# A fifth place for a split weight granule behind the token stages of a two-layer backbone

## The chip, the cores and the metric

One core of a Trainium2 chip runs the whole program. The metric is the device time of one execution in microseconds (us); lower is better. Between two kernels a difference under about 0.2% cannot be told from none here.

## The reference, cut to what matters

```python
def conv_ffn(h, w_in, conv_w, w_out):
    g, v = jnp.split(h @ w_in, 2, axis=-1)
    g = dwconv(g, conv_w)                    # three taps along the tokens
    return (jax.nn.silu(g) * v) @ w_out

for l in range(DEPTH):                       # DEPTH = 2; layer 0 even, layer 1 odd
    ...
    y, yc = even_mixer(...) if l % 2 == 0 else odd_mixer(...)   # input product, mixers, output product
    x = x + mod[2] * rms_norm(y, mix_post_g[l])
    h = modulate(rms_norm(x, ffn_pre_g[l]), mod[3], mod[4])
    x = x + mod[5] * rms_norm(conv_ffn(h, ffn_w_in[l], ffn_conv_w[l], ffn_w_out[l]), ffn_post_g[l])
    ...                                      # the 256 context tokens likewise, in layer 0 alone
```

All is float32: D_MODEL 1024, 512 latent and 256 context tokens, feed-forward width 2816. Layer 0 works on 768 tokens, layer 1 after its input product on 512.

## The kernel before

**Products in three terms.** Each float32 operand is split into a high part in the format fp32r and a low part, the rest. A product is high*high + high*low + low*high on TensorE. The split of a weight granule (128 partitions x 1024 numbers, 512 KB) takes two instructions: ScalarE copies `raw` into `w_hi` (`take_high`, L1089, semaphore `w_high`), then VectorE subtracts into `w_lo` (`take_low`; its instruction is recorded under the helper `vt`, L1506, as all VectorE tensor_tensor work; semaphore `w_low`, `low` in the code).

**Places.** Loads land in two raw buffers: granule n in `raw[:, n % 2]`. The split parts have four places, granule n in number n % 4. So three things are ordered: `load(n)` on the SP queue waits until the low part of n-2 is taken; `take_high(n)` must come behind the last product that read granule n-4; TensorE waits for `low` before it uses n. SP, ScalarE and VectorE go through the granules strictly in order, between their other work.

**Units.** A unit is a product of 256 output columns over all of D_MODEL; it uses two granules (part 0 and part 1, four k-tiles each) and one of two PSUM sets. `product` (L670) runs a unit over all tokens. Feed-forward units come in pairs: the gate half g (copied to `gpad`, then three taps on VectorE, L1967 and L1965) and the value half v (multiplied in, split into `hid_hi`, `hid_lo`). In `ffn` each engine does, for a pair: copy and taps, then the split of the two granules of the next pair's first unit (`unit_high(n + 4)`, `unit_low(n + 4)`), then the other half, then two more granules.

**Token stages and edges.** `token_products` (L724) computes an output product: tokens on the partitions, two halves `a` of 512 columns, `half` = 4 granules each (3 for down02 and down12). Four of these stages are edges: out0, down02, out1, down12. In the second half of an edge TensorE goes tile by tile (128 tokens); behind each tile ScalarE squares, VectorE normalizes, adds to x, normalizes again (`xn`, L1561), TensorE transposes (`turn`, L710), and ScalarE and VectorE modulate and split into `h_hi`, `h_lo`. GpSimd takes part at down02 and down12 (L2155). The next product begins before the last tiles are through: `first_products` (L696) takes the first two units of the next phase (up00, in1, up10) in token segments of 256: segment 0 for unit 0, a `turn`, segment 0 for unit 1, then segment 1 for both, and so on. All four granules of these two units must stay in their places to the last segment.

**Order of the splits at an edge.** With n the edge's first granule, `edge` on ScalarE and VectorE takes granule n + half + 3 between the two halves. When the last tile comes, it takes the next two (n + half + 4 and + 5), ahead of that tile's squares and sums. Behind the last tile's sums it takes the rest, to n + 2 half + 3. At out0 and out1 the four granules of up00 (up10) are n + 8 to n + 11, so their first two are taken at the last tile and the others behind it. At down02 the first granule of in1 is n + half + 3 already, the second and third are taken at the last tile, the fourth behind it. The third unit's granules (up00 + 4 and + 5) follow in `ffn`, behind the first unit's taps.

Of the kernel before, what the change touches and what calls it, by code (L numbers as in the profile page):

```python
# [34 lines left out]
P = 128  # L35
# [87 lines left out]
def token_stages():  # L123
# [3 lines left out]
    for name, nt, ktiles in (("out0", NT, KD), ("down00", NT, 8), ("down01", NT, 8), ("down02", NT, 6),  # L127
# [27 lines left out]
SEGMENTS = (((0, 0, 1, None), (0, 1, 3, FIRST), (1, 0, 1, SECOND), (1, 1, 3, THIRD), (2, 0, 1, FOURTH), (2, 1, 2, None)),  # L155
            tuple((g, 0, size // 2, None) for g, size in enumerate(FFN_GROUPS)))
TokenStage = namedtuple("TokenStage", "nt half edge tiles granules sums squares chain")
# [34 lines left out]
def build(nc, a, out):  # L192
# [3 lines left out]
    with ctx:  # L196
# [30 lines left out]
        W_LO = at[0]  # L227
        w_lo = place("w_lo", [P, 4, 4, 256], F32R)
        ident = place("ident", [P, P])
        ones = place("ones", [P, P])  # L230
# [11 lines left out]
        ada_w = place("ada_w", [P, 4, 2, 512])  # L242
        ada_acc = place("ada_acc", [P, 512])
        A0 = at[0]
        ARENA = top // 32 * 32 - A0
        assert ARENA >= 83960, ARENA

# [39 lines left out]
        ada_m = place("ada_m", [P, 2, 4, 256], offset=RAW)  # L287
        ada_c = place("ada_c", [P, 3, 512], offset=A0 + 36864)
        ada_d = place("ada_d", [P, 512], offset=SCR + 8192)
        ada_r = place("ada_r", [P, 512], offset=SCR + 8192)  # L290
        sums_even = [[ada_acc[:, :], ada_c[:, 0, :]], [ada_c[:, 1, :], ada_c[:, 2, :]]]
        sums_of = [ada_acc[:, :], ada_d[:, :]]
# [66 lines left out]
        w_ffn_out = [a["ffn_w_out"][l].rearrange("(k p) n -> p k n", p=P) for l in range(2)]  # L359
        w_ada = [a["ada_w"][l].rearrange("(k p) n -> p k n", p=P) for l in range(2)]  # L360

        def bank(s_, m, h):
# [315 lines left out]
        def first_products(pe, u, n, rhs, segs, ready, between):  # L678

            for e, (t0, t1) in enumerate(segs):  # L680
                for x in range(2):
                    s = (u + x) % 2
                    if not e:
                        psum_free(pe, u + x)
                    for part in range(2):
                        m_ = n + 2 * x + part
                        if not e:
                            pe.wait_ge(low, m_ + 5)
                        if not x and not part:
                            ready(e)  # L690
                        for kk in range(4):
                            k = 4 * part + kk
                            for m in range(2):
                                c = slice(m * P, (m + 1) * P)
                                for q, (w, x_) in enumerate(((w_hi, rhs[0]), (w_hi, rhs[1]), (w_lo, rhs[0]))):
                                    last = nc.tensor.matmul(acc[:, s, m, t0:t1], w[:, m_ % 4, kk, c], x_[:, k, t0:t1],  # L696
                                                            start=(k == 0 and q == 0), stop=(k == KD - 1 and q == 2))
                    if e == len(segs) - 1:
                        last.then_inc(unit_done, 1)
                    between(2 * e + x)  # L700
# [379 lines left out]
        def _(act):  # L1080
# [3 lines left out]
            def take_high(n, i=0):  # L1084

                if n >= N_GRANULES:
                    return
                act.wait_ge(raw_full[n % 2], loaded(n, i))
                nc.scalar.activation(w_hi[:, n % 4], raw[:, n % 2], ACT.Copy).then_inc(high, 1)  # L1089

# [66 lines left out]
            def edge(name, l, comp):  # L1157
# [9 lines left out]
                granule_used(act, name, half - 1)  # L1167
                take_high(n + half + 3)
                act.wait_ge(y_eps, EDGES.index(name) + 1)
                for j in range(nt):  # L1170
                    if j == nt - 1 and on:
                        for g in range(2):
                            granule_used(act, name, half + g)
                            take_high(n + half + g + 4)
                    y_squares(name, 1, j)
                    q = t.chain + j
                    act.wait_ge(y_square, t.squares + nt + j + 1)
                    nc.scalar.activation(yroot[:, 0, j:j + 1], ysq[:, j, 1:2], ACT.Sqrt, bias=ysq[:, j, 0:1]).then_inc(y_root, 1)
                    if not on:
                        continue  # L1180
                    if j >= behind:
                        tile_half(name, j - behind, l, comp)
                    act.wait_ge(x_new, q + 1)
                    x_squares(j, NT + q, junk_x[:, :])
                    if j >= behind:
                        tile_high(name, j - behind)
                if on:
                    for g in range(2, half):
                        granule_used(act, name, half + g)
                        take_high(n + half + g + 4)  # L1190
                    for j in range(nt - behind, nt):
                        tile_half(name, j, l, comp)
                        tile_high(name, j)
# [199 lines left out]
            def ffn(l, tokens):  # L1393
# [4 lines left out]
                for g, off, count, chunks in SEGMENTS[l]:  # L1398
                    with turns(act, count) as i:
                        u, n, pair = U[f"up{l}{g}"] + 2 * off, G[f"up{l}{g}"] + 4 * off, first_pair + sum(FFN_GROUPS[:g]) // 2 + off  # L1400
                        psum_full(act, u, i)

# [5 lines left out]
                        last.then_inc(set_free[u % 2], 1)  # L1408
                        unit_high(n + 4, i)
                        u, n = u + 1, n + 2  # L1410
# [90 lines left out]
        def _(dve):  # L1501
# [31 lines left out]
            def take_low(n, i=0):  # L1533

                if n < N_GRANULES:
                    dve.wait_ge(high, n + 1 + 4 * i)
                    vt(w_lo[:, n % 4], raw[:, n % 2], w_hi[:, n % 4].bitcast(F32), ALU.subtract).then_inc(low, 1)

# [96 lines left out]
            def edge(name, l, comp, rows_in):  # L1635
# [14 lines left out]
                for j in range(nt):  # L1650
                    summed(name, 2, 0, j)
                take_low(n + half + 3)
                dve.wait_ge(y_square, t.squares + nt)
                nc.vector.tensor_scalar(ysq[:, 0:nt, 0], ysq[:, 0:nt, 0], EPS, None, ALU.add).then_inc(y_eps, 1)
# [3 lines left out]
                for j in range(nt):  # L1658
                    if j == nt - 1 and on:
                        unit_low(n + half + 4)  # L1660
                    summed(name, 2, 1, j)
# [26 lines left out]
                if not mixer:  # L1688
                    nc.vector.memset(poolw[:, :, :], 0.0).then_inc(sem("poolw_zero"), 1)
                    normed(nt - 1)  # L1690
                    tile_low(name, nt - 3)
                for m in range(2, half):
                    take_low(n + half + m + 4)
                for j in range(nt - (1 if mixer else 2), nt):
# [244 lines left out]
            def ffn(l, tokens):  # L1939
# [5 lines left out]
                for g, off, count, chunks in SEGMENTS[l]:  # L1945
                    tile, pair = sum(FFN_GROUPS[:g]) + 2 * off, FT // 2 * l + sum(FFN_GROUPS[:g]) // 2 + off
                    with turns(dve, count) as i:
                        sd.loop(i, 5 + 4 * len(chunks or ()))
                        u, n = U[f"up{l}{g}"] + 2 * off, G[f"up{l}{g}"] + 4 * off
                        if chunks:  # L1950
                            dve.wait_ge(unit_done, u + 2 * i)
                            for e in range(2):
                                ada_sums(chunks[e], sums_of[e:], i)
                        psum_read(dve, u, i)
                        for w in range(3):
                            for m in range(2):
# [13 lines left out]
                                else:  # L1970
                                    sd.done(ins)
                        unit_low(n + 4, i)
                        u, n = u + 1, n + 2
# [227 lines left out]
```

## Time and profile before

| | us |
|---|---|
| median of 3 runs | 1716.85 |
| lowest, highest | 1715.59, 1717.81 |
| profiled execution, its own time | 1718.76 |
| span of its instructions | 1717.0 |

The profiled execution lies 1.91 above the median of the runs. TensorE is busy for 1625.7 us of the span, VectorE for 1023.8, ScalarE for 555.2, GpSimd for 54.7. Its mean granted clock is 0.977 of full speed. Windows and timelines are in us from the start of the span.

### The profile page before, as it was taken

To read this page: it belongs to the slowest core of one execution; us is meant where nothing else is said; L and a number is where in the kernel's file an instruction comes from. 1 tells how busy PE (TensorE), PEld (TensorE's weight loads), DVE (VectorE), ACT (ScalarE), POOL (GpSimd) and SP (SyncE) were. 2 spreads that over 40 slices of the span, in tenths; PEclk is the share of its full clock that TensorE was granted. 3 is DMA by queue.
4 is the path that set the end of the run, shared out by engine and by line. 5 is a ranking of instruction groups with operands and counts; after the bars stand their busy time and mean duration, and the time that the engine had idled before them with its cause. 6 is when DMAs were issued, how large, how long until landed. Compare 5 with 4: busy or idle time off the path is not lost.

```text
span 1717.0 us, 21965 instructions
## 1 busy us (share of the span) xinstructions
PE 1625.7 (95%) x8698; PEld 1358.3 (79%) x8698; DVE 1023.8 (60%) x1448; ACT 555.2 (32%) x883; POOL 54.7 (3%) x74
## 2 busy tenths in 40 slices
PE   6999999886899999999999999899899999999998
PEld 2688887675788887888888887788677888888886
DVE  2899995653675766467734444754783644344344
ACT  2313215472262321023210323631433543233233
POOL 0400000110000000000000000100000000000001
PEclk9999999988899999999999999899999999999999
DMA  9422221304314454444424132131001233233222
GB/s 300 137 62 69 59 70 44 130 25 86 111 50 147 147 168 162 132 161 161 160 85 148 50 98 62 65 99 49 25 1 50 74 98 111 86 98 111 75 95 87
DMA packets 134009, 169.43 MB, mean 99 GB/s; under 512 B 15970, under 2 KB 92450, under 8 KB 133930
## 3 DMA queue, kind: packets, MB, share of 16 engines
q1 hardware_dynamic: 133360, 168.11, 30.8%
q8 instruction: 55, 0.90, 0.2%
q10 hardware_dynamic: 570, 0.22, 0.1%
q14 instruction: 24, 0.20, 0.0%
HBM read 166.17 MB, written 2.15 MB: 98 GB/s over the span
## 4 chain that ended last, share of the span: by engine, by line
PE 81%; DVE 8%; ACT 4%; issue 2%; DMA 1%; POOL 1%; POOLq 0%; DVEq 0%; SPq 0%; ACTq 0%
PE acc L670 47%; PE acc L724 19%; PE acc L696 3%; PE acc L875 2%; PE acc L1071 2%; PE acc L1050 2%; PE acc L776 1%; DVE w_lo L1506 1%; PE acc L1018 1%; PE acc L641 1%; PE acc L910 1%; DVE y L1506 1%; DMA ada_w<-in_ada_w 1%; DVE x L1673 1%; POOL y L2155 1%
## 5 line engine op out<-in xcount | busy, mean ns | idle before, releaser
L670 PE MATMUL acc<-h_hi,w_hi 128*128 128x512 f32 (+1 forms) x1424 | 417.7, 354 | 7.4 <-DVE w_lo L1506 4.4
L670 PE MATMUL acc<-h_lo,w_hi 128*128 128x512 f32 (+1 forms) x1424 | 412.8, 351 | 0.0
L670 PE MATMUL acc<-h_hi,w_lo 128*128 128x512 f32 (+1 forms) x1424 | 412.2, 351 | 0.0
L1506 DVE TENSOR_TENSOR w_lo<-raw,w_hi 128x1024 fp32r<-128x1024 f32 x186 | 222.8, 1229 | 155.7 <-ACT w_hi L1089 155.7
L1089 ACT ACTIVATE w_hi<-raw 128x1024 fp32r<-128x1024 f32 x186 | 189.1, 1055 | 259.3 <-PE acc L724 222.7
L670 PEld LDWEIGHTS acc<-h_hi,w_hi 128*128 128x128 f32 x1424 | 230.5, 189 | 45.2 <-DVE w_lo L1506 4.8
L670 PEld LDWEIGHTS acc<-h_lo,w_hi 128*128 128x128 f32 x1424 | 231.3, 189 | 39.4 <-issue 0.5
L670 PEld LDWEIGHTS acc<-h_hi,w_lo 128*128 128x128 f32 x1424 | 229.8, 189 | 38.3
L724 PE MATMUL acc<-w_hi,hid_hi 128*128 128x512 f32 x440 | 175.7, 399 | 0.0
L724 PE MATMUL acc<-w_hi,hid_lo 128*128 128x512 f32 x440 | 175.0, 398 | 0.0
L724 PE MATMUL acc<-w_lo,hid_hi 128*128 128x512 f32 x440 | 175.0, 398 | 0.0
L1774 DVE SCALAR_TENSOR_TENSOR conv_u<-conv_u,dw_w 128x783 f32<-128x783 f32 x120 | 124.1, 1034 | 4.0
L1967 DVE TENSOR_SCALAR hid<-gpad,ffn_cw 128x512 f32 (+1 forms) x66 | 25.2, 438 | 131.1 <-ACT gpad L1407 131.1
L724 PEld LDWEIGHTS acc<-w_hi,hid_lo 128*128 128x128 f32 x440 | 83.2, 189 | 20.4
L724 PEld LDWEIGHTS acc<-w_lo,hid_hi 128*128 128x128 f32 x440 | 83.3, 189 | 20.0
L724 PEld LDWEIGHTS acc<-w_hi,hid_hi 128*128 128x128 f32 x440 | 83.2, 189 | 19.9
L1506 DVE TENSOR_TENSOR hid<-hid,acc 128x1024 f32 (+2 forms) x22 | 32.7, 1488 | 107.8 <-ACT mods L1105 59.5
L1965 DVE SCALAR_TENSOR_TENSOR hid<-gpad,ffn_cw,hid 128x512 f32 (+3 forms) x132 | 77.5, 656 | 0.0
L1105 ACT ACTIVATE mods<-acc,vec 128x1 f32 (+2 forms) x72 | 14.5, 262 | 191.4 <-PE acc L641 191.1
L696 PE MATMUL acc<-h_hi,w_hi 128*128 128x256 f32 x224 | 65.9, 294 | 10.7 <-DVE w_lo L1506 9.3
L724 PE MATMUL acc<-w_hi,h_hi 128*128 128x512 f32 x160 | 65.5, 409 | 6.0 <-DVE small L1937 3.3
L1527 DVE SCALAR_TENSOR_TENSOR ada_acc<-ada_w,cond,ada_acc 128x512 f32<-128x512 f32 x91 | 68.2, 750 | 4.0
(234 smaller groups left out, 2048.6 us busy)
## 6 DMA issues: line engine op xcount, KB each, us to landing
ada_w<-in_ada_w SPq DMA_DIRECT2D x88, 512.0 KB, 5.8
raw<-in_ffn_w_in SPq DMA_DIRECT2D x88, 512.0 KB, 3.7
raw<-in_ffn_w_out SPq DMA_DIRECT2D x44, 512.0 KB, 4.5
raw<-in_even_w_in SPq DMA_DIRECT2D x24, 512.0 KB, 4.5
ada<-in_ada_w SPq DMA_DIRECT2D x8, 1024.0 KB, 12.1
raw<-in_odd_w_in SPq DMA_DIRECT2D x12, 512.0 KB, 3.9
raw<-in_even_w_out SPq DMA_DIRECT2D x8, 512.0 KB, 4.7
ada_m<-in_ada_w SPq DMA_DIRECT2D x8, 512.0 KB, 3.9
```

Source lines behind the costliest of these rows:

```text
L670: last = nc.tensor.matmul(acc[:, s, m, t0:t1], w[:, slot, kk, c], x_[:, k, t0:t1], start=(k == 0 and q == 0), stop=(k == KD - 1 and q == 2))
L696: last = nc.tensor.matmul(acc[:, s, m, t0:t1], w[:, m_ % 4, kk, c], x_[:, k, t0:t1], start=(k == 0 and q == 0), stop=(k == KD - 1 and q == 2))
L724: last = nc.tensor.matmul(tile_bank(name, a, j), x_[:, k, j * P:(j + 1) * P], w[:, m_ % 4, 2 * kk:2 * kk + 2, :].rearrange("p a c -> p (a ...
L875: last = nc.tensor.matmul(dst, probs[e % 4][:, t * P - t0:t * P - t0 + P], v_tok[:, ORDER[q], hd, :], start=(q, d, t) == FIRST_TOUCH[b], s ...
L1050: last = nc.tensor.matmul(acc[:, 0, n % 2, t0:t1], inb[:, 2 + hd, i * P:(i + 1) * P], kT[:, hd // 3, t0:t1], start=True, stop=True)
L1071: last = nc.tensor.matmul(acc[:, 1, 1, c:c + P], v1[:, j, (hd // 3) * HD:(hd // 3 + 1) * HD], pT[:, n % 2, j * P:(j + 1) * P], start=(j == ...
L1089: nc.scalar.activation(w_hi[:, n % 4], raw[:, n % 2], ACT.Copy).then_inc(high, 1)
L1506: return nc.vector.tensor_tensor(out_, in0, in1, op)
L1527: ins = nc.vector.scalar_tensor_tensor(of[e], w, scale, of[e], ALU.mult, ALU.add)
L1774: ins = nc.vector.scalar_tensor_tensor(dst, src, tap, dst, ALU.mult, ALU.add)
L1965: ins = nc.vector.scalar_tensor_tensor(dst, src, c, dst, ALU.mult, ALU.add)
L1967: ins = nc.vector.tensor_scalar(dst, src, c, None, ALU.mult)
```

## The change

A fifth place `w_edge` (high and low part) is added beside the four. Three granules, the set `early`, use it: the first of up00, the second of in1, the first of up10. Each is taken between the two halves of its edge, right behind granule n + half + 3. At the last tile the edge then takes the granules n + half + 5 up to n + 2 half + 2 (two at out0 and out1, one at down02), and one behind the last tile. As up00's and up10's first granule does not stand in the four places, the third unit's first granule has its place free while the first pair is at work; `ffn` takes it ahead of its first pair's work, and only the third unit's second granule is left behind the taps. To make room `ada_acc` moves over scratch space, `sums_even` lies wholly in `ada_c`, and the program's dynamic_dma_scratch_size goes from 8192 to 1024.

```diff
-            tuple((g, 0, size // 2, None) for g, size in enumerate(FFN_GROUPS)))
+            ((0, 0, 1, None), (0, 1, FFN_GROUPS[0] // 2 - 1, None))
+            + tuple((g, 0, size // 2, None) for g, size in enumerate(FFN_GROUPS) if g))
...
+        w_edge = place("w_edge", [P, 2, 4, 256], F32R)
...
-        ada_acc = place("ada_acc", [P, 512])
...
-        ada_c = place("ada_c", [P, 3, 512], offset=A0 + 36864)
-        ada_d = place("ada_d", [P, 512], offset=SCR + 8192)
+        ada_c = place("ada_c", [P, 4, 512], offset=A0 + 36864)
+        ada_acc = place("ada_acc", [P, 512], offset=SCR + 6176)
+        ada_d = place("ada_d", [P, 512], offset=SCR + 8224)
...
-        sums_even = [[ada_acc[:, :], ada_c[:, 0, :]], [ada_c[:, 1, :], ada_c[:, 2, :]]]
+        sums_even = [[ada_c[:, 2 * q + e, :] for e in range(2)] for q in range(2)]
...
+        early = {G["up00"], G["in1"] + 1, G["up10"]}
+
+        def w_of(n):
+
+            return (w_edge[:, 0], w_edge[:, 1]) if n in early else (w_hi[:, n % 4], w_lo[:, n % 4])
...
                 granule_used(act, name, half - 1)
                 take_high(n + half + 3)
+                if on:
+                    take_high(n + half + 4)
                 act.wait_ge(y_eps, EDGES.index(name) + 1)
                 for j in range(nt):
                     if j == nt - 1 and on:
-                        for g in range(2):
+                        for g in range(1, half - 1):
                             granule_used(act, name, half + g)
                             take_high(n + half + g + 4)
...
-                    for g in range(2, half):
-                        granule_used(act, name, half + g)
-                        take_high(n + half + g + 4)
+                    granule_used(act, name, 2 * half - 1)
+                    take_high(n + 2 * half + 3)
...
+                        if n in early:
+                            take_high(n + 4)
                         psum_full(act, u, i)
...
                         last.then_inc(set_free[u % 2], 1)
-                        unit_high(n + 4, i)
+                        if n not in early:
+                            take_high(n + 4, i)
+                        take_high(n + 5, i)
...
                 take_low(n + half + 3)
+                if on:
+                    take_low(n + half + 4)
...
                     if j == nt - 1 and on:
-                        unit_low(n + half + 4)
+                        for m in range(1, half - 1):
+                            take_low(n + half + m + 4)
...
-                for m in range(2, half):
-                    take_low(n + half + m + 4)
+                take_low(n + 2 * half + 3)
...
+                        if n in early:
+                            take_low(n + 4)
                         psum_read(dve, u, i)
...
-                        unit_low(n + 4, i)
+                        if n not in early:
+                            take_low(n + 4, i)
+                        take_low(n + 5, i)
...
-    nc = bacc.Bacc("TRN2", target_bir_lowering=False, num_devices=1, dynamic_dma_scratch_size=8192)
+    nc = bacc.Bacc("TRN2", target_bir_lowering=False, num_devices=1, dynamic_dma_scratch_size=1024)
```

`first_products`, `take_high` and `take_low` now address the places through `w_of`. The SP queue's code is unchanged.

## Rows read from the trace of the kernel before

**Rows 1.** TensorE's waits over the span: total us, times, longest

```profile
PE acc L651 <- DVE ada_d L1527: 9.9, 2, 7.7
PE acc L696 <- DVE w_lo L1506: 9.3, 5, 3.9
PE acc L670 <- DVE w_lo L1506: 4.4, 2, 2.7
```

**Rows 2.** Chain that ended last around out0 and up00: start, us, what

```profile
497.09 2.27 DVE w_lo L1506 x2
...
503.19 0.75 DVE xn L1561
...
505.08 1.15 DVE w_lo L1506
506.36 23.29 PE acc L696 x192
...
536.91 1.15 DVE w_lo L1506
...
538.10 18.75 PE acc L670 x96
...
575.17 17.06 PE acc L670 x96
```

**Rows 3.** Timeline, up00's third unit, TensorE and the gate copy before it

```profile
529.72 1.51 ACT L1407 ACTIVATE gpad<-acc 128x1024 f32<-128x1024 f32 x2 [20.00 <-PE acc L696]
538.10 0.50 PE L670 MATMUL acc<-h_hi,w_hi 128*128 128x512 f32 x1 [2.71 <-DVE w_lo L1506]
```

**Rows 4.** Windows of up00's third unit, its own matmuls: us, busy (x), clock, DMA share, GB/s

```profile
538.50:541.90 3.40, 3.40 (x13) 2.92 (x12) 0.50 0.67 208
541.90:545.30 3.40, 3.40 (x21) 2.93 (x20) 1.00 1.02 346
```

**Rows 5.** Timeline between the halves of out0 (VectorE, ScalarE) and of out1 (ScalarE)

```profile
463.47 0.16 DVE L1654 TENSOR_SCALAR small<-small 128x6 f32<-128x6 f32 x1
465.35 0.60 ACT L1147 ACTIVATE junk<-acc 128x512 f32<-128x512 f32 x1 [7.01 <-PE acc L724]
...
1320.58 0.60 ACT L1147 ACTIVATE junk<-acc 128x512 f32<-128x512 f32 x1 [3.85 <-PE acc L724]
```

**Rows 6.** Timeline at up10, TensorE behind two of its waits, and the gate copy

```profile
1348.90 0.35 PE L696 MATMUL acc<-h_hi,w_hi 128*128 128x256 f32 x1 [1.16 <-DVE w_lo L1506]
1362.04 1.03 ACT L1407 ACTIVATE gpad<-acc 128x1024 f32<-128x1024 f32 x1
1368.06 0.50 PE L670 MATMUL acc<-h_hi,w_hi 128*128 128x512 f32 x1 [1.66 <-DVE w_lo L1506]
```

**Rows 7.** Timeline at down02, the splits of in1's four granules, and TensorE

```profile
1059.45 1.23 DVE L1506 TENSOR_TENSOR w_lo<-raw,w_hi 128x1024 fp32r<-128x1024 f32 x1 [1.74 <-ACT w_hi L1089]
1095.12 2.36 DVE L1506 TENSOR_TENSOR w_lo<-raw,w_hi 128x1024 fp32r<-128x1024 f32 x2 [2.16 <-ACT w_hi L1089]
1096.40 0.58 PE L696 MATMUL acc<-h_hi,w_hi 128*128 128x256 f32 x1 [3.93 <-DVE w_lo L1506]
1106.18 1.22 DVE L1506 TENSOR_TENSOR w_lo<-raw,w_hi 128x1024 fp32r<-128x1024 f32 x1
1107.45 0.39 PE L696 MATMUL acc<-h_hi,w_hi 128*128 128x256 f32 x1 [1.85 <-DVE w_lo L1506]
```

**Rows 8.** Chain that ended last through down02

```profile
1060.76 4.21 DVE y L1506 x7
```

**Rows 9.** Windows at in1: us, PE, PEld, DVE, ACT, POOL, clock, DMA, GB/s

```profile
1096.40:1101.70 5.30, 5.29 (x25) 5.30 (x26) 4.16 (x7) 2.42 (x7) 2.30 (x1) 0.50 0.73 227
1107.45:1112.00 4.55, 4.54 (x25) 4.55 (x26) 2.45 (x5) 1.06 (x1) 0.00 (x0) 0.62 0.70 233
```

**Rows 10.** Window of the program's start, columns as in rows 9

```profile
10.00:42.00 32.00, 25.00 (x123) 12.18 (x123) 11.48 (x22) 10.91 (x26) 0.00 (x0) 1.00 1.01 325
```

**Rows 11.** DMA issues of the whole span: count, KB each, median us to landing

```profile
raw<-in_ffn_w_in SPq DMA_DIRECT2D x88, 512.0 KB, 3.7
```

More of the change, by code:

```diff
@@ L242, in build @@
         ada_w = place("ada_w", [P, 4, 2, 512])
-        ada_acc = place("ada_acc", [P, 512])
         A0 = at[0]
         ARENA = top // 32 * 32 - A0
-        assert ARENA >= 83960, ARENA
+        assert ARENA >= 84000, ARENA
         qkov = place("qkov", [P, 16, T], offset=A0)
@@ L694, in first_products @@
                                 c = slice(m * P, (m + 1) * P)
-                                for q, (w, x_) in enumerate(((w_hi, rhs[0]), (w_hi, rhs[1]), (w_lo, rhs[0]))):
-                                    last = nc.tensor.matmul(acc[:, s, m, t0:t1], w[:, m_ % 4, kk, c], x_[:, k, t0:t1],
+                                for q, (w, x_) in enumerate(((0, rhs[0]), (0, rhs[1]), (1, rhs[0]))):
+                                    last = nc.tensor.matmul(acc[:, s, m, t0:t1], w_of(m_)[w][:, kk, c], x_[:, k, t0:t1],
                                                             start=(k == 0 and q == 0), stop=(k == KD - 1 and q == 2))
@@ L1088, in take_high @@
                 act.wait_ge(raw_full[n % 2], loaded(n, i))
-                nc.scalar.activation(w_hi[:, n % 4], raw[:, n % 2], ACT.Copy).then_inc(high, 1)
+                dst = w_of(n)[0]
+                nc.scalar.activation(dst, raw[:, n % 2], ACT.Copy).then_inc(high, 1)
             def unit_high(n, i=0):
@@ L1536, in take_low @@
                     dve.wait_ge(high, n + 1 + 4 * i)
-                    vt(w_lo[:, n % 4], raw[:, n % 2], w_hi[:, n % 4].bitcast(F32), ALU.subtract).then_inc(low, 1)
+                    hi, lo = w_of(n)
+                    vt(lo, raw[:, n % 2], hi.bitcast(F32), ALU.subtract).then_inc(low, 1)
             def unit_low(n, i=0):
```

## Prediction

> **What bounds the kernel now.** I read the page first: TensorE is busy for 1625.7 of the 1717.0 us, so only its waits and the stretches at its lower clock can be won back. Then its waits [rows 1]: for the low part of a weight granule it waits 9.3 us in five places in `first_products` and 4.4 us in two in `product`; the other large one there (`ada_d`, the sums for adaLN columns) this edit does not touch. The timelines at the three edges show where they are. At up00 the wait ahead of the second unit is seen in the chain: low part at 505.08, TensorE on at 506.36 [rows 2], behind 1.2 us of idleness (the `turn` was over at about 505.2); a like wait stands before the first unit. Then comes 2.71 us ahead of the third unit [rows 3]. At up10 they are 1.16 ahead of the second unit and 1.66 ahead of the third [rows 6]; the first unit has the fifth of the five, 9.3 - 1.2 - 1.16 - 3.93 - 1.85 = 1.2. At in1 they are 3.93 in the middle of unit 0 and 1.85 in the middle of unit 1 [rows 7]. The windows give the clock: right behind the 2.71 us wait TensorE is granted 0.50 (the 1.2 GHz level) for 3.4 us, with 13 matmuls of one of the three terms where the next 3.4 us at 1.00 (2.4 GHz) hold 21 [rows 4]; at in1 it is 0.50 behind the 3.93 us wait and 0.62 behind the 1.85 us wait [rows 9].
>
> **The change at up00.** (1) up00's first granule is split right behind out0's last. Cost: one ScalarE copy (about 1.05) and one subtraction (1.15, [rows 2]) between the halves. VectorE had put the epsilon in at 463.47, and ScalarE began the second half's squares at 465.35, when TensorE delivered the tile [rows 5]: the cover is 465.35 - 463.47 - 0.16 = 1.7 us, so 1.15 costs nothing; without that cover it would cost 1.15. (2) At the last tile two granules are split as before, now the second and third. The last tile's squares, sums and `xn` (ready at 503.19 + 0.75 = 503.94, [rows 2]) keep their times. Unit 0 may begin 1.2 earlier, at about 497.1, but its 48 matmuls end by 502.9, and then the `turn` of the last tile waits for `xn` at 503.94. Before, that turn began at 504.16; so of the first 1.2 us only 0.15 is kept, which I leave out. (3) The third granule is there by 499.4, so unit 1 begins when the turn is over: the 1.2 us wait at 506.36 is gone. Unit 1 needs the fourth granule 2.9 us later, at about 508.1; it is now alone behind `xn` and `h_lo`, ready at 505.08 + 1.15 = 506.2 [rows 2]. Gain 1.2. (4) From there TensorE runs through to the end of segment 2 (535.4 before). The third unit's first granule is taken by both engines at the start of `ffn`, some 25 us ahead; its load needs place 0 of `raw`, free at 499.4, and lands within about 3.7 us [rows 11]. The PSUM set is free when the gate copy ends, 529.72 + 1.51 = 531.2 [rows 3], 4 us ahead. So the 2.71 us go. The second granule stays behind the taps: 536.91 before, one place earlier and shifted by 1.2 with TensorE, ready near 536.9; the unit reaches it after half its 16.75 us, near 542.6. Gain 2.7. (5) The clock: with no idleness from 505 on there is nothing for the fall at 538.5 to follow. At the full clock the 13 matmuls take 13/21 of 3.4 = 2.1, so the stretch costs 3.4 - 2.1 = 1.3 by this count; by time at half the clock it is 1.7. The unit took 18.75 us against 17.06 for the next pair's first [rows 2], a difference of 1.7, and I take that. Sum at up00: 1.2 + 2.7 + 1.7 = 5.6.
>
> SP's queue: granules load in the old order, only sooner: the third by 34 us, as the first's low part now falls in the pause, the fourth by 1.1, the third unit's second half by about 30. The two loads behind the taps come about 1.2 (one subtraction) and 1.2 (TensorE's shift) earlier, and the adaLN weights behind them with them. From here to down02 TensorE has one wait, in down00 (9.9 - 7.7 = 2.2 us, [rows 1]), for VectorE's sums for the adaLN columns, which begin behind TensorE's own last unit and so move with it. So the 5.6 us reach down02 whole.
>
> **At up10**, the same with 4 tiles: between the halves of out1 ScalarE stands idle for 3.85 us [rows 5], more than the copy and the subtraction one after the other (2.2). The wait of 1.16 goes; the wait of 1.66 goes, since the gate copy ends at 1362.04 + 1.03 = 1363.1 [rows 6] and TensorE reaches the third unit at 1368.06 - 2.8 = 1365.2. The wait ahead of the first unit is again taken up by the turn of the last tile. Gain 1.16 + 1.66 = 2.8. The clock stayed at 1.00 there, nothing to win. In the following pair the load of the third unit's fourth granule is issued when the taps are over, as before, and is not waited for. TensorE has no wait from 1368 to the last product.
>
> **At down02 and in1** the cover is missing. The chain runs through the very place where the second granule is now put: low part of the first at 1059.45, then the gating product at 1060.76 [rows 7, 8] (seven pieces without a pause), and from there through ScalarE, GpSimd and VectorE tile by tile to 1101. The subtraction moves all of this by 1.15. In exchange, at the last tile one granule is split and not two (1095.12, 2.36 for the two, [rows 7]), which gives 1.13 back ahead of the last sum: everything behind it, and the fourth granule at 1106.18, keeps its time. TensorE now runs through the first 3.93 us wait, but then waits for `xn` of the next-to-last tile, computed behind that last sum, and at last for the same fourth granule: unit 1's second part begins at 1107.45 as before. Gain 0. Its last wait grows from 1.85 to about 4.6 us, so the low clock behind it comes as before [rows 9]: 24 matmuls in 4.5 us where 2.9 would do, both times. Bounds: -1.6 if the clock stays up this time, +1.7 if one more stretch of 3.4 us at 0.50 falls behind 1107.45, +1.15 more if the last tile does not give back its part.
>
> **Other parts.** The places of `ada_acc`, `ada_c`, `ada_d` are scratch of other stages at times when those are over; no instruction is added: 0. Reading `w_edge` and not `w_hi` in the same matmuls: 0 (what TensorE does per matmul has no term for the place in any row). The smaller DMA scratch: see the last rival.
>
> **Sum.** 5.6 + 2.8 + 0 = 8.4 us. Against the profiled execution, 1718.76 - 8.4 = 1710.4; the median of the runs lies 1.91 lower, 1716.85 - 8.4 = **1708.4**.
>
> The Trainium skill, "TensorE: Matmul & The Clock Gate", section on what is actually happening, says that the gate's watching is not tied to the kernel's start, so where the clock turns varies from run to run. This trace, being one, can neither show nor deny it. By that rule the 1.7 us at up00 was lost in some runs of the median only, and the gain would be between 6.7 and 8.4.
>
> **Rivals.** (a) *The clock takes part of it back.* Shifted by 5.6 us, the idle stretches at in1 (now some 2.7 and 4.6 us) and the one in down00 meet the clock otherwise: one or two further stretches of 1.7 us, or the 1.7 at up00 not won in the median. For it: the drops behind waits of 1.85 and 2.71 us [rows 4, 9]. Time: 8.4 - 1.7 to 8.4 - 3.4 less than before, 1710.1 to 1711.8. (b) *in1 gains too*: somewhere the chain from 1060.76 to 1095 has slack, the 1.15 is absorbed, and the last tile starts 1.13 earlier, with the lower clock of [rows 9] gone: another 1.1 + 1.6, 1705.7. Against it: the chain passes without a pause of its own. (c) *The third unit does not start earlier*: not the split but the taps' neighbour, the freeing of the set or a load not landed, holds it. Then only the two waits of 1.2 go, 2.4 us, 1714.5, within 0.2%. Against it: the copy at 531.2 and a load free since 499.4. (d) *Slower, by the DMA scratch*: if the loads' descriptors pass through the scratch, an eighth of it slows all loads. Loads set the pace in the start, 32 us at a DMA share of 1.01 [rows 10]. It decides the sign where they grow by 8.4/32 = 26%; at 50% they cost 16, giving 1716.85 - 8.4 + 16 = 1724.5. Elsewhere a unit of 17 us needs two loads of 3.7 [rows 11] and has room. Against it: the loads are on the hardware queue q1, and GpSimd issues none.
>
> **How the numbers follow.** Forecast 0.60 (its own range 1707.0 to 1710.0: 1.3 against 1.7 for the clock, 0.15 twice for the turns, and the spread of the runs). (a) 0.20, (b) 0.07, (c) 0.07, (d) 0.06. The range reaches to (b) on one side and over (a) on the other with the 1.15 of in1 added: 1705.5 to 1713.0; (c) and (d), 0.13, lie outside. Faster by over 0.2% (3.4 us, what a measurement can tell): forecast, (a), (b) = 0.87. Within: 0.07. Slower: 0.06.
>
> **What would show it.** TensorE's waits for `w_lo`: the two in `product` gone, the ones in `first_products` down from five to one (in1, about 4.6 us), with waits of about 1 us for `xn` ahead of the last turn at up00 and up10. Third unit of up00 with no idle time and 21 matmuls of a term in every 3.4 us. At down02 the gating product 1.15 later, measured from the half's last sum, the last sum of the edge at its old distance. The first 42 us unchanged. Wrong would be: a wait ahead of the third unit named otherwise; in1's fourth granule earlier or later; a longer landing of the loads.

## The result and the profile after

| | before | after |
|---|---|---|
| median of the runs, us | 1717.19 (5) | 1708.19 (5) |
| lowest, highest | 1715.59, 1719.53 | 1707.60, 1709.33 |
| span of the profiled execution | 1717.0 | 1707.6 |

The ratio is 0.9939, 95% interval 0.9926 to 0.9953: faster, and by 9.0 us in the medians, where 8.4 were forecast (1708.4). The two medians divide to 0.9948, which lies inside the interval. In a later measurement, on chip 15, the same kernel took 1708.88 against 1716.86 (0.9956, 0.9941 to 0.9971).

TensorE's waits in the kernel after, over the span (the answer to [rows 1]; total us, times, longest):

```profile
PE acc L659 <- DVE ada_d L1541: 9.0, 2, 6.9
PE acc L718 <- DVE xn L1576: 8.6, 5, 3.1
PE acc L704 <- DVE w_lo L1520: 4.5, 1, 4.5
```

The two waits for `w_lo` in `product` are gone, and of the five in `first_products` (L704 now) one is left. The waits for `xn` in front of a `turn` (L718) have grown and taken up part of them: 8.6 us in five places, where before had 3.0 us in two:

```profile
PE acc L710 <- DVE xn L1561: 3.0, 2, 2.0
```

The chain that ended last, around up00, answers to [rows 2]:

```profile
501.88 0.76 DVE xn L1576
502.64 0.04 issue
502.69 1.09 PE acc L718 x8
503.78 28.80 PE acc L704 x240
532.58 16.96 PE acc L678 x96
```

and the timelines of TensorE's last wait there and of what lies between the halves of out0 (VectorE, ScalarE) answer to [rows 3, 5]:

```profile
502.69 1.09 PE L718 MATMUL acc<-ident,xn 128*128 128x128 f32 x8 [1.16 <-DVE xn L1576]
...
462.13 1.21 DVE L1520 TENSOR_TENSOR w_edge<-raw,w_edge 128x1024 fp32r<-128x1024 f32 x1
463.26 0.16 DVE L1671 TENSOR_SCALAR small<-small 128x6 f32<-128x6 f32 x1
...
464.00 0.60 ACT L1156 ACTIVATE junk<-acc 128x512 f32<-128x512 f32 x1 [6.07 <-DVE small L1671]
```

From the last `turn` on TensorE is one piece to the end of the third unit, 240 matmuls and then 96. The new subtraction of 462.13 is over at 463.34, and VectorE's epsilon behind it at 463.42, ahead of the tile that ScalarE takes at 464.00. The profile names the epsilon for this start, but it had been done for 0.6 us; from TensorE's first matmul of the half to ScalarE's first square it is 1.74 us before and after (465.35 - 463.61 and 464.00 - 462.26). So the cover of 1.7 us held. The third unit's windows (us, TensorE busy, its weight loads, clock, DMA share, GB/s; compare [rows 4]) have no stretch at half the clock:

```profile
536.50:539.90 3.40, 3.40 (x21) 2.94 (x20) 1.00 0.99 304
539.90:543.30 3.40, 3.40 (x21) 2.94 (x21) 1.00 1.02 382
```

At up10 the chain is likewise one piece behind the turn, where [rows 6] had two waits:

```profile
1340.54 1.09 PE acc L718 x8
1341.63 17.28 PE acc L704 x144
1358.91 41.28 PE acc L678 x182
```

At down02 and in1, timeline of VectorE's splits and of TensorE (answers to [rows 7]):

```profile
1050.55 1.23 DVE L1520 TENSOR_TENSOR w_lo<-raw,w_hi 128x1024 fp32r<-128x1024 f32 x1 [1.74 <-ACT w_hi L1098]
1051.70 1.22 DVE L1520 TENSOR_TENSOR w_edge<-raw,w_edge 128x1024 fp32r<-128x1024 f32 x1
...
1090.09 1.09 PE L718 MATMUL acc<-ident,xn 128*128 128x128 f32 x8 [2.51 <-DVE xn L1576]
...
1098.55 0.58 PE L704 MATMUL acc<-h_hi,w_hi 128*128 128x256 f32 x1 [4.51 <-DVE w_lo L1520]
```

The 3.93 us wait of [rows 7] has become one of 2.51 us for `xn`, and the wait for the fourth granule is 4.51 us. From the first granule's low part to unit 1's second part it is 1098.55 - 1050.55 = 48.0 us, as before (1107.45 - 1059.45 = 48.0). The windows around it and in the odd mixer that follows (us; busy and count of TensorE, its weight loads, VectorE, ScalarE, GpSimd; clock, DMA share, GB/s):

```profile
1087.50:1092.00 4.50, 1.99 (x18) 1.92 (x18) 3.70 (x6) 2.41 (x7) 2.00 (x1) 1.00 0.02 5
1098.55:1102.50 3.95, 3.95 (x18) 3.95 (x19) 2.45 (x5) 1.06 (x1) 0.00 (x0) 0.50 0.84 268
1174.50:1177.90 3.40, 3.40 (x10) 2.20 (x10) 0.55 (x2) 0.23 (x1) 0.00 (x0) 0.50 0.02 5
1177.90:1181.30 3.40, 3.40 (x13) 2.54 (x12) 1.85 (x3) 0.00 (x0) 0.00 (x0) 0.50 0.00 0
1201.80:1205.20 3.40, 3.11 (x9) 2.08 (x10) 2.81 (x6) 3.29 (x5) 0.00 (x0) 0.50 0.00 0
```

Behind the wait for `xn` the clock stays at 1.00, behind the one for the granule it is 0.50 (as in [rows 9]), and in the mixer three stretches of 3.4 us stand at 0.50, where the profiled execution of before has one:

```profile
1183.60:1187.00 3.40, 3.40 (x7) 1.43 (x6) 0.55 (x2) 0.23 (x1) 0.00 (x0) 0.50 0.02 5
```

Put together from the start of one stage's first matmul to the next's, in the two profiled executions. "Attention" is here, and in all that follows, the stage from the odd mixer's value product to its first attention scores; the 70.7 us of attention behind it are the same in all traces and stand under "all else".

| stage | before | after | saved |
|---|---|---|---|
| start, layer 0 up to the turns of out0 | 463.61 | 462.26 | 1.35 |
| out0's second half, up00 to unit 1 | 42.75 | 41.28 | 1.47 |
| up00, unit 1 to the third unit | 31.73 | 28.88 | 2.85 |
| third unit and its partner | 36.94 | 35.31 | 1.63 |
| the rest of layer 0's FFN | 456.72 | 455.15 | 1.57 |
| turns of down02, in1 to unit 1's second part | 75.69 | 75.69 | 0.00 |
| the rest of in1 and the projections behind it | 66.19 | 66.56 | -0.37 |
| attention | 48.69 | 51.04 | -2.35 |
| out1's second half, up10 to unit 1 | 55.89 | 54.58 | 1.31 |
| up10, unit 1 to the third unit | 19.17 | 17.36 | 1.81 |
| all else | 419.62 | 419.49 | 0.13 |
| span | 1717.0 | 1707.6 | 9.4 |

Five of the rows with a gain are the prediction's. The 1.57 in the rest of the FFN was not in it, the -2.35 in attention was there as a rival, and the 1.35 of the start is of the size by which executions of one kernel differ there (462.26 and 460.87 us in the two traces of the kernel after).

### The profile page after: what moved, and what is told of

Read it like the earlier page. It is cut to its first block, busy times and chain, and to the rows that moved or that the text cites. A ratio compares the mean times of both kernels' runs of the same rounds, so it can differ in the third digit from the quotient of the medians.

```text
span 1707.6 us, 21913 instructions
## 1 busy us (share of the span) xinstructions
PE 1621.4 (95%) x8698; PEld 1356.7 (79%) x8698; DVE 1023.9 (60%) x1448; ACT 546.3 (32%) x876; POOL 54.3 (3%) x74
## 2 busy tenths in 40 slices
DMA packets 134010, 169.43 MB, mean 99 GB/s; under 512 B 15971, under 2 KB 92451, under 8 KB 133931
## 3 DMA queue, kind: packets, MB, share of 16 engines
q1 hardware_dynamic: 133360, 168.11, 31.1%
## 4 chain that ended last, share of the span: by engine, by line
PE 82%; DVE 7%; ACT 4%; issue 2%; DMA 1%; POOL 1%; POOLq 0%; SPq 0%; DVEq 0%; ACTq 0%
PE acc L678 47%; PE acc L732 19%; PE acc L704 4%; PE acc L883 2%; PE acc L1079 2%; PE acc L1058 2%; PE acc L784 1%; PE acc L1026 1%; PE acc L649 1%; DMA ada_w<-in_ada_w 1%; PE acc L918 1%; DVE w_lo L1520 1%; DVE x L1691 1%; POOL y L2176 1%; DVE y L1520 1%
## 5 line engine op out<-in xcount | busy, mean ns | idle before, releaser
L1520 DVE TENSOR_TENSOR hid<-hid,acc 128x1024 f32 (+3 forms) x22 | 32.7, 1488 | 107.0 <-ACT mods L1114 54.6
L883 PEld LDWEIGHTS acc<-v_tok,probs 128*128 128x128 f32 x336 | 47.2, 221 | 24.4 <-DVE probs L1892 12.3
L1541 DVE SCALAR_TENSOR_TENSOR ada_d<-ada_w,cond,ada_d 128x512 f32<-128x512 f32 x84 | 62.9, 749 | 4.6 <-DMA ada_w<-in_ada_w 2.6
```

The lines of the kernel that those rows point to most:

```text
L883: last = nc.tensor.matmul(dst, probs[e % 4][:, t * P - t0:t * P - t0 + P], v_tok[:, ORDER[q], hd, :], start=(q, d, t) == FIRST_TOUCH[b], s ...
L1520: return nc.vector.tensor_tensor(out_, in0, in1, op)
L1541: ins = nc.vector.scalar_tensor_tensor(of[e], w, scale, of[e], ALU.mult, ALU.add)
```

## The experiments

**Scratch alone.** Does the smaller DMA scratch slow the loads (rival (d)), and does it have a part in layer 0's faster FFN?

```diff
-    nc = bacc.Bacc("TRN2", target_bir_lowering=False, num_devices=1, dynamic_dma_scratch_size=8192)
+    nc = bacc.Bacc("TRN2", target_bir_lowering=False, num_devices=1, dynamic_dma_scratch_size=1024)
```

> The kernel before with nothing changed but dynamic_dma_scratch_size, 8192 to 1024. Theory 1 (the loads do not pass through the scratch): 1717.2 as before, the start from 10 to 42 us at the same DMA share, loads landing in 3.7 us. Theory 2 (they do): slower by 8 us and more, longer landings. Theory 3 (the trace of after has about 1.7 us less in layer 0's units between 540 and 1050 than my sum, because two matmuls of 512 and 256 columns take 347 ns there and not 353; that comes from where things lie in SBUF, which the scratch shifts): about 1715.5, and the units of layer 0's loops take 16.75 and not 17.06.

Measured: 1718.68 against 1717.97, ratio 1.0008 (0.9999 to 1.0017). The start's window, columns as in [rows 10], has the same share and rate:

```profile
10.00:42.00 32.00, 24.84 (x126) 12.26 (x127) 11.48 (x22) 10.79 (x26) 0.00 (x0) 1.00 1.01 325
```

Loads of `in_ffn_w_in` land in 3.6 us (3.7 before, [rows 11]). Rival (d) falls: the scratch shows no cost (the interval leaves room for 0.17%, 2.9 us, where the rival had 8.4 and more), and it gives nothing either; the slower units of layer 0 took 17.06 us as before.
**The third unit's first granule behind the taps again.** The rest of after stays.

```diff
-                        if n in early:
-                            take_high(n + 4)
                         psum_full(act, u, i)
...
-                        if n not in early:
-                            take_high(n + 4, i)
-                        take_high(n + 5, i)
+                        unit_high(n + 4, i)
```

and likewise on VectorE.

> The changed kernel, but the third unit's first granule is split behind the taps again, at up00 and at up10. Theory 1 (the terms of the prediction stand alone): up00's third unit waits about 2.7 us again and the clock falls to 0.50 behind it in most runs (1.7), up10's waits about 1.7: 6.0 us over the changed kernel, 1714.2; only the two waits of 1.2 stay won. Theory 2 (the wait is for the PSUM set or for a load): no change against 1708.2.

Measured: 1711.91, ratio 0.9967 (0.9954 to 0.9979), so 1.9 to 4.8 us above after by the two ratios of after. The wait and the low clock behind it are back at up00 (timeline of TensorE; the granted clock is 0.51 from 533.60 to 537.00):

```profile
532.81 0.62 PE L678 MATMUL acc<-h_hi,w_hi 128*128 128x512 f32 x2 [2.71 <-DVE w_lo L1516]
533.27 0.51 PE L678 MATMUL acc<-h_lo,w_hi 128*128 128x512 f32 x2
533.62 0.80 PE L678 MATMUL acc<-h_hi,w_lo 128*128 128x512 f32 x2
```

Unit 1 to the third unit takes 31.74 us and the next pair 36.93, both as before: together 4.5 us above after, the two terms 2.7 and 1.7 of the prediction. At up10, however, there was no wait, and the stage took 17.63 us, not 19.17. Something else had won that 1.66.

**The loop split alone.** In before's profile a row stands ahead of up10's gate copy that the prediction did not quote, an activation table load of 1.28 us; in after it is gone:

```profile
1360.75 1.28 ACT L1407 ACT_TABLE_LOAD   x1 [8.49 <-PE acc L696]
1362.04 1.03 ACT L1407 ACTIVATE gpad<-acc 128x1024 f32<-128x1024 f32 x1
```

The edit splits the first pair of layer 1 off the loop and does nothing else:

```diff
-            tuple((g, 0, size // 2, None) for g, size in enumerate(FFN_GROUPS)))
+            ((0, 0, 1, None), (0, 1, FFN_GROUPS[0] // 2 - 1, None))
+            + tuple((g, 0, size // 2, None) for g, size in enumerate(FFN_GROUPS) if g))
```

> Before with one edit, the loop split at layer 1 (its first pair of units outside the loop). Theory: the table load at up10 goes and unit 1 to the third unit takes 17.6 us instead of 19.17; layer 0 keeps its 140.93 and 169.74 us; 1717.0 - 1.55 = 1715.5. Rival: the wait there is for the fifth granule alone, 19.17 us stay and the time is 1717.0. Second rival: the faster pairs of layer 0 come from the changed code and not from the layout; then 140.25 us show here too and the time is 1713.8.

Measured: 1717.58 against 1718.41, ratio 0.9994 (0.9981 to 1.0008). By itself the time cannot be told from none; the trace can. ScalarE's timeline in this kernel:

```profile
1359.10 1.03 ACT L1408 ACTIVATE gpad<-acc 128x1024 f32<-128x1024 f32 x1 [8.48 <-PE acc L697]
1360.02 2.00 ACT L1090 ACTIVATE w_hi<-raw 128x1024 fp32r<-128x1024 f32 x2
1362.03 1.28 ACT L1414 ACT_TABLE_LOAD   x1
1363.72 1.06 ACT L1414 ACTIVATE hid<-hid 128x1024 f32<-128x1024 f32 x1 [0.41 <-DVE hid L1966]
```

and in the kernel of the next experiment, which has before's loops:

```profile
1357.41 1.28 ACT L1407 ACT_TABLE_LOAD   x1 [8.49 <-PE acc L696]
1358.71 1.03 ACT L1407 ACTIVATE gpad<-acc 128x1024 f32<-128x1024 f32 x1
1359.63 2.00 ACT L1089 ACTIVATE w_hi<-raw 128x1024 fp32r<-128x1024 f32 x2
1363.65 1.28 ACT L1413 ACT_TABLE_LOAD   x1 [2.02 <-DVE hid L1965]
```

With the split the copy follows TensorE at once, the two splits come 1.28 earlier against the product's end, and the third unit waits no more: 17.62 us for the stage, against 19.17 (the cause of the wait at up10 was the late copy, and with it the late splits). The Trainium skill, "ScalarE: Activation LUTs", section on what a table load costs, gives 1283 ns for the load and about as much again for a drain; here the load has those 1.28 us, but the copy starts 1.30 us behind the load's start and the whole stage gained 1.55, so the second part is not seen. Over the span seven table loads fewer are made (883 ScalarE instructions before, 876 after), all from the two lines of this loop. Layer 0's slower units kept their 17.06 us, so the second rival falls; down01's stage took 141.24 us, 0.3 more than before, all of it in its first unit (16.96 for 16.65), as in the kernel with the scratch alone.

**The ada sums moved alone.** In after six of the units of layer 0's FFN, pairs of matmuls of 512 and 256 columns, are shorter by 0.3 us. The edit moves `ada_acc` and the fourth `ada_c` (and `ada_d` by 32 bytes) as in after; no fifth place, old scratch, old loops:

```diff
-        ada_acc = place("ada_acc", [P, 512])
-        ada_c = place("ada_c", [P, 3, 512], offset=A0 + 36864)
-        ada_d = place("ada_d", [P, 512], offset=SCR + 8192)
+        ada_c = place("ada_c", [P, 4, 512], offset=A0 + 36864)
+        ada_acc = place("ada_acc", [P, 512], offset=SCR + 6176)
+        ada_d = place("ada_d", [P, 512], offset=SCR + 8224)
...
-        sums_even = [[ada_acc[:, :], ada_c[:, 0, :]], [ada_c[:, 1, :], ada_c[:, 2, :]]]
+        sums_even = [[ada_c[:, 2 * q + e, :] for e in range(2)] for q in range(2)]
```

> Before with one edit: ada_acc and the fourth ada_c moved as in after, with no fifth place, the old scratch and the old loops; 2 KB fewer stand ahead of the arena. Theory: the faster pairs of layer 0 (347 ns, down01's stage 140.25 us) come with the places of the ada sums, and the time is 1717.0 - 1.6 = 1715.4. Rival: they come from the addresses of the weights or the hidden matrices, which the fifth place shifts by 8 KB; then 140.93 us and 1717.0 stay.

Measured: 1715.00, ratio 0.9981 (0.9970 to 0.9992). The chain's rows where [rows 2] has a unit of 17.06 us, and of the next unit:

```profile
575.38 16.75 PE acc L670 x96
592.13 0.79 PE acc L641 x8
592.92 16.75 PE acc L670 x96
```

down01's stage took 140.25 us and down02's 169.43, as in after (before: 140.93 and 169.74). The rival, the weights' addresses, falls: the fifth place is not here. The kernels with after's scratch alone and with after's loops alone kept 17.06. The edit also shifts what lies behind `ada_acc` by 2 KB, so whether the place of the sums does it or that shift is open.

**Layout and loops together, nothing early.** After with one edit on the side of the places; the order of the splits at all three edges is that of before (this part of the edit is not shown).

```diff
-        early = {G["up00"], G["in1"] + 1, G["up10"]}
+        early = {}
```

> The memory layout of after (the fifth place, left unused, the moved sums, the small scratch) and its loop split at layer 1, with no granule early. Theory: a row of the profile that the prediction did not have, the activation table load ahead of the gpad copy at up10, goes with the loop split (unit 1 to the third unit there 17.6 us instead of 19.17), and the paired matmuls of layer 0's FFN run at 347 ns instead of 350 to 356 because of where things lie (down01's stage 140.25 us instead of 140.93, down02's 169.43 instead of 169.74). With before at 1717.0 that makes about 1717.0 - 1.6 - 1.6 = 1713.8. Rival: both come with the early granules alone, and this kernel takes 1716.5 to 1717.5 with stages of 19.17 and 140.93 us.

Measured: 1714.94, ratio 0.9973 (0.9964 to 0.9983), with stages of 17.61, 140.25 and 169.43 us. That is 3.5 us less than before in the medians, 4.6 by the ratio and 3.1 (1.56 and 1.57) by the stages. So 3 to 5 of the 9.0 us have nothing to do with when a granule is split.

**One edge early at a time.** Layout and loops of after, and in `early` only up00's granule, only in1's, only up10's, or the two outside in1. The first of these edits; an edge that is not in `early` has the order of before:

```diff
-        early = {G["up00"], G["in1"] + 1, G["up10"]}
+        early = {G["up00"]}
```

> The changed kernel with the fifth place used at up00 alone; down02 and out1 in the order of before. Theory 1 (5.6 of the 8.4 us are at up00): 1717.2 - 5.6 = 1711.6; waits of 1.2, 1.2 and 1.7 us at up10 again. Theory 2 (the clock term is not won in the median, or is made up elsewhere): 1713.3.

> After with the early granule at up10 alone. By the traces so far: out1's turn shorter by 0.9, unit 1 shorter by 0.4, unit 1 to the third unit 17.36 instead of 17.62 (0.26): 1.6 under the layout kernel of this group, so 1713.8 - 1.6 = 1712.2; up00 keeps 34.74 and 31.73 us. The prediction's own sum would have 1.16 + 1.66 = 2.8 from the early granule alone and so 1711.0.

> The changed kernel with the fifth place used at in1 alone; out0 and out1 in the order of before, no third unit early. Theory 1 (in1's edit is worth nothing): 1717.2 less the 1.6 us that up10 gains without its granule, as the run with the third unit late showed (the first pair of layer 1 stands outside the loop and its copy has no table load ahead of it): 1715.6. Theory 2 (the longer idleness of TensorE at in1 costs more clock): 1717 to 1719.

> The changed kernel without in1's early granule: at down02 the order of before, at out0 and out1 the new one. Theory 1 (the subtraction added between the halves is given back at the last tile, and the fourth granule sets in1's time): 1708.2, the same as changed; at in1 waits of 3.9 and 1.85 us as before, and from the first split between the halves to unit 1's second part 48.0 us both times. Theory 2 (in1's edit costs by the longer idleness and the clock): 1706.5. Theory 3 (it gains): 1710 to 1711.

| early | us | ratio (interval) | unit 1 to third unit, up00 / up10 | attention |
|---|---|---|---|---|
| none | 1714.94 | 0.9973 (0.9964 to 0.9983) | 31.73 / 17.61 | 48.70 |
| up00 | 1707.57 | 0.9946 (0.9933 to 0.9960) | 28.87 / 17.62 | 48.21 |
| up10 | 1712.19 | 0.9963 (0.9949 to 0.9977) | 31.72 / 17.36 | 51.07 |
| in1 | 1716.01 | 0.9991 (0.9982 to 1.0000) | 31.73 / 17.61 | 51.07 |
| up00, up10 | 1705.01 | 0.9922 (0.9908 to 0.9935) | 28.87 / 17.35 | 48.69 |
| all three (again) | 1708.88 | 0.9956 (0.9941 to 0.9971) | 28.88 / 17.36 | 51.10 |

The rows "in1" and "all three" were measured on chip 15, the others on chip 13. up00's granule alone took 1707.57 where 1711.6 was expected; the expectation had nothing for layout and loops, which give 3 to 5 us in all of these kernels. up10's met its 1712.2, and in1's came to 1716.01 for 1715.6. up00's granule is worth 0.0027 of the time, 4.6 us, in the ratios and 1.4 + 2.9 + 1.4 = 5.7 in the stages of its trace; up10's 1.7 and 1.5. in1's granule seems to cost: 0.0018 (3.1 us) added to nothing early, and some 0.0026 (the mean of after's two ratios less 0.9922, 4.4 us) added to the other two. By the traces it is 2.8 and 2.7 us, nearly all in attention. The intervals overlap at their ends or nearly touch, and the kernels stood on different chips, so a loss is likely and its size loose. Up to unit 1's second part the sum is the same with it and without it (75.69 and 75.67), as forecast; the loss lies behind.

**The fourth granule of in1 at the last tile too.** The prediction had this granule as what TensorE waits for at in1. At down02 it is now split at the last tile, ahead of the sums, and none behind:

```diff
-                        for g in range(1, half - 1):
+                        for g in range(1, half - (name[:3] == "out")):
...
-                    granule_used(act, name, 2 * half - 1)
-                    take_high(n + 2 * half + 3)
+                    if name[:3] == "out":
+                        granule_used(act, name, 2 * half - 1)
+                        take_high(n + 2 * half + 3)
```

and likewise on VectorE.

> The changed kernel; at down02 the fourth granule of in1 is split at the last tile too, together with the third, not behind the last tile's sums. TensorE has left down02 some 7 us before ScalarE comes to the last tile there, and the granule's load has long landed, so nothing holds it. Theory 1 (only the place in the order keeps in1 waiting): the last sum is 1.15 later, the turn of the next-to-last tile too; unit 1's second part begins some 3 us earlier and no turn waits long; in1's second segment starts about 4 to 5 us earlier, 1703.5. Theory 2 (the last tiles' own chain through GpSimd and VectorE sets the second segment's start whatever the granules do): the added 1.15 ahead of it counts, 1709.3.

> The changed kernel itself, so that the others of this call have it on the same chip. 1708.2; the run without in1's early granule gave 1705.0 on another chip, so in1's edit either costs 2 to 3 us by the clock (then the in1-only kernel shows it as well), or that was chance and this one gives 1705 to 1706 too.

Measured on one chip: 1702.65 (0.9915, 0.9900 to 0.9929) against after's 1708.88 (0.9956), the best of all versions. TensorE's two largest waits that bear on this and its last wait at in1:

```profile
PE acc L659 <- DVE ada_d L1542: 9.3, 2, 7.2
PE acc L718 <- DVE xn L1577: 8.7, 4, 3.6
...
1093.54 1.09 PE L718 MATMUL acc<-ident,xn 128*128 128x128 f32 x8 [3.65 <-DVE xn L1577]
```

No wait for a `w_lo` is left in `product` or `first_products` (one of 1.0 us in `token_products` stays as in before), though the tile's `xn` is one subtraction later. To unit 1's second part it is 73.67 us, 2.0 less; the next stage takes 15.50 and not 17.57 (its low stretch is gone), and attention 48.68 and not 51.10. Only the 2.0 us are sure to be the edit's: the low stretch was missing too in two kernels with the fourth granule late (15.59 us with up00's granule alone and with the sums moved alone), and attention took 48.7 us in others as well.

**And the third granule at out0 and out1 behind the last tile's normalization.** On top of that version:

```diff
-                        for g in range(1, half - (name[:3] == "out")):
+                        for g in range(1, 2 if name[:3] == "out" else half):
...
+                    if j == nt - 1 and name[:3] == "out":
+                        granule_used(act, name, half + 2)
+                        take_high(n + half + 6)
```

and likewise on VectorE.

> As the kernel with in1's fourth granule early, and at out0 and out1 only the second granule of up00 (up10) is split ahead of the last tile's squares and sums; the third one behind that tile's normalization, ahead of the low part of the tile before. Theory 1 (the turn of the last tile waits for the normalization, which stands behind both splits): it comes 1.1 us earlier at either edge, unit 1's granule is there when the turn is over: 2.2 us less than the kernel it is built on, 1701.3. Theory 2 (the granule is then what comes late): the same time as that kernel, the wait named for the low part again.

Measured: 1703.54 (0.9927, 0.9913 to 0.9940). The wait for `xn` ahead of the turn is gone at both edges (from unit 0's first matmul to unit 1's it takes 7.22 us where it took 7.99 at up00, and 6.86 for 7.62 at up10): 1.5 us by the trace, not to be seen in the median beside runs that spread by 8 us (1698.17 to 1706.22). The two kernels cannot be told apart, so neither theory is decided by the time; by the trace theory 1 holds, with 1.5 for its 2.2 us.

## Why the prediction came out, step by step

- **up00, first wait (0.15 left out), second wait (1.2).** Right; together 1.47. The turn for the last tile does wait for `xn`, 1.16 us, as step (2) said.
- **up00, the third unit (2.7).** Right: 2.85, and undoing that one split brought 2.71 back.
- **up00, the clock (1.7).** Right: 1.63. One reading of its rows was wrong without harm: the 13 and 21 of [rows 4] count all matmuls of the stretch, not those of one term. The Trainium skill, "TensorE: Matmul & The Clock Gate", section on what is actually happening, by which the clock's turns vary from run to run, would have made this a gain in some runs only. Here all eight traces with the wait (before's among them) had a stretch at 0.50 and none of the six without it did, so whether the clock fell did not vary at this place; how much it cost did, 1.4 to 2.9 us by the length of the third unit. At in1 the traces bear the rule out (see the last section).
- **The covers between the halves.** Right at out0 and, by the same distances, at out1. No wait for a load came up.
- **up10 (1.16 + 1.66).** The size is right (1.31 and 1.81), the reason only half. The second term was put down to the early granule, while the loop split, which the prediction listed in no step, wins 1.55 of it without any granule early. That the number came out is luck to this extent. With both in, the early granule adds 0.26 there. "no instruction is added: 0" missed that instructions fall away.
- **in1 (0).** Right in mechanism and number to the granule wait; the gating product moved by 1.13 us against the first granule's low part (1052.90 - 1050.55 = 2.35 us for 1060.67 - 1059.45 = 1.22), TensorE's wait for the first tile's `xn` grew from 1.96 to 3.08 us, and the last tile gave it back. The fourth granule set the time, and taking that wait away won 2.0.
- **Other parts (0).** Wrong. Where the sums of the adaLN columns lie, or what that shifts, is worth 1.6 us by the stages and 3.3 by the ratio (1.4 at the least).
- **Rival (a).** It came in beside the forecast, at a place it did not name: not in down00 or in1 but in attention, +2.35 us (in1 itself took 0.37 more). The four traces that have in1's granule early and its fourth one late all show 49.9 to 51.1 us there; of the eight with none early at in1, seven show 48.2 to 48.7; with the fourth moved as well, 48.7 and 47.7. That it is the longer idleness at in1 which brings it about fits this count but is not shown: one kernel without it (up10 alone) had 51.07 too, in an execution that took 1719.17 us, 7.0 above that kernel's median.
- **Rival (b)** fell (75.69 both times), **(c)** fell (no wait ahead of the third unit), **(d)** fell (scratch alone).

So the sum of 8.4 met 9.0 partly by luck: the five terms gave 9.1 instead of 8.4 in the traces, the unforeseen 1.6 and the clock's -2.7 took off 1.1, and the start's 1.35, which is within what executions differ by, put it back. Of the 9.1 some 1.55 belong to the loop split.

## What to carry to other kernels

An operand's preparation that stands behind a chain can be bought early with one more buffer, and it pays where the buffer's split falls into a pause of both engines; inside a chain it only exchanges one wait for another, until the last late operand is moved too. Count what an edit of loops and places does to instructions that nobody wrote, table loads above all, and try the layout alone: here that was a third of the gain or more. When several edges are changed alike, measure each alone; the one at in1 won nothing, and probably lost, until its fourth granule followed.

## What the runs showed of the hardware that was not expected

- Activation table loads of 1.28 us stood ahead of both the gate copy and the silu in all four passes of layer 1's first loop, and in none of its later two loops. With the first pass outside the loop one of these eight is left, ahead of the first silu.
- A unit of pairs of matmuls of 512 and 256 columns took 17.06 us in six places of layer 0's FFN in one layout and 16.75 in another, with the same work; the other units did not change, but for one that went from 16.65 to 16.95. Why is open.
- Behind the 2.71 us at up00 TensorE was always granted 0.50, the 1.2 GHz level, for one or two stretches of 3.4 us. At in1 the same pause did not always have the same end. Behind the 2.51 us for `xn` it was granted 1.00 in three traces (the window from 1087.50 above is one), and 0.50 for 3.2 us in the fourth, that of the third unit's granule behind the taps (from 1093.64). Behind the wait for the fourth granule it fell in ten traces, at pauses of 1.73 to 4.52 us, and stayed at 1.00 in two, at pauses of 1.39 us (up00 alone) and 2.92 us (the sums moved alone; 1.00 from 1106.07 to 1110.00). The length of the pause alone does not tell whether the clock falls.
